# One tile for the residual instead of two, read with a stride by the gather, and an earlier load into the tile that comes free

## The reference, cut to what matters

```python
h = rmsnorm(x, attn_norm_g)
x = x + hybrid_mixer(h, ...)          # ends in concat(...) @ w_out, (256, 2048) @ (2048, 2048)
h = rmsnorm(x, ffn_norm_g)
x = x + hier_moe(h, ...)              # router, then for each expert e its tokens:
                                      #   (silu(h @ w_gate[e]) * (h @ w_up[e])) @ w_down[e], weighted
return rmsnorm(x, final_norm_g)
```

## Time and profile before

| what | us |
|---|---|
| median of 3 runs (lowest 1422.26, highest 1424.28) | 1424.24 |
| profiled execution, first to last instruction (the span; this is also its own time as it was kept) | 1421.9 |
| TensorE busy in it | 1220.1 |
| VectorE busy | 489.9 |
| ScalarE busy | 256.4 |

### The profile page before, as it was taken

One profiled execution on the slowest core, in us unless ns is written; L12 is line 12 of the kernel. 1 busy time (PEld: TensorE's weight loads), 2 busy tenths in 40 slices (PEclk: granted clock), 3 DMA queues, 4 the chain that ended last, 5 costly groups with the idle time before them and its releaser, 6 DMA issues.

```text
span 1421.9 us, 18013 instructions
## 1 busy us (share of the span) xinstructions
PE 1220.1 (86%) x7475; PEld 711.4 (50%) x7475; DVE 489.9 (34%) x1013; ACT 256.4 (18%) x629; POOL 18.3 (1%) x84
## 2 busy tenths in 40 slices
PE   8999999999999998769689958769687686876976
PEld 7999999776568753223244314214242242422422
DVE  5599987663875431121110220111101111011113
ACT  3001111444600132011111102002020020200212
POOL 2000000000010000000000000000000000000001
PEclk9999999999999999789899988979889898898999
DMA  9958567431644899999999999999999999999996
GB/s 300 323 176 173 152 151 238 118 86 34 178 108 163 352 410 428 428 428 427 428 426 429 427 428 428 428 428 427 428 428 428 426 428 428 427 427 428 427 428 261
DMA packets 133363, 479.35 MB, mean 337 GB/s; under 512 B 47804, under 2 KB 105632, under 8 KB 107552
## 3 DMA queue, kind: packets, MB, share of 16 engines
q1 hardware_dynamic: 126816, 477.58, 86.2%
q10 hardware_dynamic: 6464, 0.58, 0.4%
HBM read 476.05 MB, written 2.10 MB: 336 GB/s over the span
## 4 chain that ended last, share of the span: by engine, by line
PE 55%; DMA 42%; DVE 1%; ACT 1%; issue 1%; POOLq 0%; POOL 0%; ACTq 0%; DVEq 0%
DMA ring<-in_expert_w_up_dram 35%; PE PS L1136 14%; PE PS L1456 10%; DMA spare<-in_expert_w_up_dram 6%; PE PS L1278 5%; PE PS L1443 4%; PE PS L1178 3%; PE PS L1255 2%; PE PS L1646 2%; PE PS L1434 1%; PE PS L1230 1%; PE PS L1656 1%; PE PS L956 1%; PE PS L1128 1%; PE PS L1197 1%; PE PS L1518 1%
## 5 line engine op out<-in xcount | busy, mean ns | idle before, releaser
L1456 PE MATMUL PS<-ring,XG 128*32 128x512 f32 x1296 | 231.2, 758 | 131.8 <-DMA ring<-in_expert_w_up_dram 91.3
L1456 PEld LDWEIGHTS PS<-ring,XG 128*32 128x32 f32 x1296 | 57.5, 134 | 264.5 <-issue 261.3
L2904 DVE TENSOR_TENSOR x<-PS,x 128x1024 f32<-128x1024 f32 x41 | 50.2, 1225 | 221.1 <-PE PS L1535 219.8
L3088 DVE TENSOR_TENSOR hTe<-PS,sg 128x128 f32<-128x128 f32 (+1 forms) x31 | 9.9, 319 | 337.5 <-ACT sg L2206 337.3
L1443 PE MATMUL PS<-ring,XG 128*64 128x512 f32 x192 | 93.2, 643 | 18.2 <-DMA ring<-in_expert_w_up_dram 14.8
L2193 ACT ACTIVATE Hs<-PS 128x512 f32<-128x512 f32 x30 | 17.9, 597 | 463.2 <-PE PS L1456 338.9
L1445 PE MATMUL PS<-ring,XG 128*64 128x512 f32 x192 | 93.4, 644 | 0.0
L1535 PE MATMUL PS<-Y,SW 128*128 128x512 f32 (+2 forms) x176 | 90.7, 627 | 1.5 <-ACT ro L2302 1.5
L1456 PE MATMUL PS<-spare,XG 128*32 128x512 f32 x208 | 69.8, 833 | 22.8 <-DMA ring<-in_expert_w_up_dram 22.8
L1434 PEld LDWEIGHTS PS<-sel,xn 128*128 128x128 f32 x640 | 75.3, 191 | 12.9 <-issue 12.7
L1136 PE MATMUL PS<-hT,ring 128*128 128x128 f32 x672 | 78.8, 275 | 0.0
(11 more groups left out here) (497 smaller groups left out, 1576.3 us busy)
## 6 DMA issues: line engine op xcount, KB each, us to landing
ring<-in_expert_w_up_dram SPq DMA_DIRECT2D x53, 2048.0 KB, 23.2
ring<-in_expert_w_gate_dram SPq DMA_DIRECT2D x53, 2048.0 KB, 26.7
ring<-in_expert_w_down_dram SPq DMA_DIRECT2D x51, 2048.0 KB, 25.0
ring<-in_w_in_dram SPq DMA_DIRECT2D x17, 2048.0 KB, 12.3
spare<-in_expert_w_gate_dram SPq DMA_DIRECT2D x9, 2048.0 KB, 24.1
spare<-in_expert_w_up_dram SPq DMA_DIRECT2D x8, 2048.0 KB, 22.7
spare<-in_expert_w_down_dram SPq DMA_DIRECT2D x8, 2048.0 KB, 26.6
ring<-in_w_in_dram SPq DMA_DIRECT2D x16, 512.0 KB, 7.3
```

What stands on the lines that cost most here:

```text
L1456: mm = pe.matmul(PS[r:r + 32, 0, :], gathered_rows(q, 4 * c + j)[:, column:column + 32], weight_rows(slots[u], 4 * (c % 2) + j), start=(c ...
L2904: dve.tensor_tensor(y, new, old, ALU.add).then_inc(sc_added, 1)
```

## The change

1. `xn` is gone, and with it the eight `normed` copies, the semaphore `xn_ready` and the waits for it on TensorE and in the SP list.
2. A tile `xr` of 2 x 2048 floats takes its place in memory. x is loaded into `xr` the second time, in natural order, and the output projection is added to it there. Square sums, router transposes and the first additions of expert results read `xr`.
3. The gather reads `xr` through `token_rows(t, k)`: the same 128 values as before, now with a stride of eight floats. The overflow path does the same; it has no work with these inputs.
4. The loads: block 0 of x is issued when all scores are done (`scored`, 24 of them), since it lies over the queries; block 1 when all weighted sums are done (`pv_done`). Between the two, after `p_turned`, chunk 3 of the second expert step goes into `x1`, which is no longer needed until the additions. The entry near the router goes away, and its waits for `xn_ready` and `ffn_ssq`; `logits_done` stays.
5. The first additions of expert results read their old value from `xr` without a permutation. The tile that the warming products read is `xr`.

```diff
+SCORED = sum(HPG * (t + 1) for p, t in STEPS)
...
-        xn = sb("xn", [P, TT, DK, P])
+        xr = sb("xr", [P, TT, D])
...
+        def token_rows(t, k):
+
+            first = 1024 * (k // 8)
+            return xr[:, t, first + k % 8:first + 1024:8]
...
                 else:
+                    sp.wait_ge(scored, SCORED)
+                    sp.dma_start(xr[:, 0, :], x[0, 0:P, :]).then_inc(x_again, 16)
                     sp.wait_ge(p_turned, 2 * PAIRS_BY[-1])
-                    for t in range(TT):
-                        sp.dma_start(x1[:, t, :], x[0, t * P:(t + 1) * P, :]).then_inc(x_again, 16)
+                    load_chunk(E - STATIC + 1, 1, 3)
+                    sp.wait_ge(pv_done, PAIRS_BY[-1])
+                    sp.dma_start(xr[:, 1, :], x[0, P:2 * P, :]).then_inc(x_again, 16)
                     sp.wait_ge(out_done, TT)
...
             load_half(1, 1)
-            sp.wait_ge(xn_ready, 4 * TT)
             sp.wait_ge(logits_done, 1)
-            sp.wait_ge(ffn_ssq, 4 * TT)
             load_half(2, 1)
             load_early(roww_flat[:, 0:512], 1024)
-            load_chunk(E - STATIC + 1, 1, 3)
...
-            warm = xn[:, 0, 0:4, :].rearrange("p k n -> p (k n)")
+            warm = xr[:, 0, 0:512]
...
                             mm = pe.transpose(PS[:, 2 + f, (j % 2) * T + t * P:(j % 2) * T + (t + 1) * P],
-                                              x1[:, t, 512 * m + j:512 * (m + 1):4], ident[:, :])
+                                              xr[:, t, 512 * m + j:512 * (m + 1):4], ident[:, :])
...
             route_last()
-            pe.wait_ge(xn_ready, 4 * TT)
             keep_warm(4, 4, tile=warm)
...
-                        mm = pe.matmul(PS[:, 6 + f % 2, (k % 2) * P:(k % 2) * P + rows_of_group(q)], xn[:, t, k, :],
+                        mm = pe.matmul(PS[:, 6 + f % 2, (k % 2) * P:(k % 2) * P + rows_of_group(q)], token_rows(t, k),
                                        sel[:, t, 0:rows_of_group(q)], start=(t == 0), stop=(t == TT - 1))
...
-            def normed(m, t):
-
-                k, p = 8 * (m // 2), 64 * (m % 2)
-                dve.tensor_copy(xn[:, t, k:k + 8, p:p + 64].rearrange("t j p -> t p j"),
-                                x1[:, t, m * 512:(m + 1) * 512].rearrange("t (p j) -> t p j", j=8)).then_inc(xn_ready, 1)
...
-                dve.tensor_tensor(x1[:, t, 0:512], PS[:, v, :], x1[:, t, 0:512], ALU.add).then_inc(out_added, 1)
-                dve.wait_ge(out_added, v + 1)
-                normed(0, t)
+                dve.tensor_tensor(xr[:, t, 0:512], PS[:, v, :], xr[:, t, 0:512], ALU.add).then_inc(out_added, 1)
...
-                first = not added_by_part(n, t, cols)
-                if first:
-                    y = y.rearrange("t (p j) -> t p j", j=8)
-                    old = xn[:, t, 8 * cols:8 * cols + 8, :].rearrange("t j p -> t p j")
+                if not added_by_part(n, t, cols):
+                    old = xr[:, t, cols * 1024:(cols + 1) * 1024]
                     held = SLOT_OF.index(RESIDUAL)
                     dve.wait_ge(w_used[held % CHUNKS], held // CHUNKS + 1)
```

More of the change, by code:

```diff
@@ L540, in build @@
         ffn_root = sem("ffn_root")
-        xn_ready = sem("xn_ready")
         xn_turned = sem("xn_turned")
@@ L1429, in gather @@
                         if q == 0:
-                            mm = pe.matmul(PS[:, 6 + f % 2, (k % 2) * P:(k % 2) * P + P], xn[:, t, k, :],
+                            mm = pe.matmul(PS[:, 6 + f % 2, (k % 2) * P:(k % 2) * P + P], token_rows(t, k),
                                            sel[:, t, 0:64].unsqueeze(1).broadcast_to([P, 2, 64]),
@@ L1793, in overflow @@
                                     mm = pe.matmul(PS[:, 6 + f % 2, (k % 2) * 256:(k % 2) * 256 + SLOTS],
-                                                   xn[:, t, k, :], sel[:, t, 0:SLOTS],
+                                                   token_rows(t, k), sel[:, t, 0:SLOTS],
                                                    start=(t == 0), stop=(t == TT - 1))
@@ L2153, in _ @@
                     act.wait_ge(ffn_ssq, v)
-                act.activation(Hs[:, :], x1[:, t, m * 512:(m + 1) * 512], ACT.Square,
+                act.activation(Hs[:, :], xr[:, t, m * 512:(m + 1) * 512], ACT.Square,
                                bias=ZERO_C, accum_out=ssq[:, t, m:m + 1]).then_inc(ffn_ssq, 1)
@@ L2782, in _ @@
                 done = PRODUCTS_BEFORE + 7 * (m - 1)
-                quarters = x1[:, :, 512 * m:512 * (m + 1)].rearrange("p t (h n) -> p t h n", h=2)
+                quarters = xr[:, :, 512 * m:512 * (m + 1)].rearrange("p t (h n) -> p t h n", h=2)
                 of = [PS[:, 4 + n // 2, 256 * (n % 2):256 * (n % 2) + 256] for n in range(7)]
@@ L2805, in _ @@
                 dve.tensor_tensor(quarters[:, 0, 1, :], of[4], quarters[:, 0, 1, :], ALU.add).then_inc(part_added, 1)
-                dve.wait_ge(out_added, TT * m + 1)
-                normed(m, 1)
                 if m < 3:
@@ L2816, in _ @@
                 dve.tensor_tensor(quarters[:, 0, 1, :], of[6], quarters[:, 0, 1, :], ALU.add).then_inc(out_added, 1)
-                dve.wait_ge(out_added, TT * (m + 1))
-                normed(m, 0)
                 if m < 3:
@@ L2901, in add_scattered @@
                 new = PS[:, bank:bank + 2, :].rearrange("p a b -> p (a b)")
-                if first:
-                    new = new.rearrange("t (p j) -> t p j", j=8)
                 dve.tensor_tensor(y, new, old, ALU.add).then_inc(sc_added, 1)
```

## The result

The changed kernel takes 1441.82 us (median of 4 runs, 1441.21 to 1442.42), the kernel before 1423.49 in the runs beside it: ratio 1.0130, interval 1.0118 to 1.0141. That is 18.3 us slower, and outside the range of the prediction.

The account below looks back on a forecast made before the run. TensorE was taken to bound up to about 550 us, then the weight stream. From a span of 1421.9, minus 1.4 for the chunk plus 0.55 for the gather gave 1421.05, so a median of 1423.4 us; range 1419.2 to 1427.0.

Parts of the forecast that it names:

- The gather with a stride: First 32 gather matmuls, before the load at 505.65: strided weight loads cost 17 ns more each, 0.55 us in all.
- own sign of being wrong: The prediction called itself wrong if gather weight loads took 260 ns or more; it expected about 210.
- upper bound of 69 ns: First 32 gather weight loads: at most 69 ns more each, 2.2 us, if the strided reading adds to the 112.
- between two and four the price went up by half: Argument for full-price strided weight loads: reading gets dearer between strides of two and four floats, with no row at eight.
- rival 2: Gather where TensorE leads: strided loads add full price, 69 ns each, 1428.5 us; at 112 ns, 1436; chance 0.18.
- Two regimes, changing over near 550; later gathers hidden: Whole kernel: TensorE sets stage ends up to about 550 us, then the 428 GB/s weight stream, which hides later gathers.
- New place of the chunk: 0: Chunk issued at 384.44 lands by 393.1, block 1 of x about 396, 14 us before need: 0 us.
- The old place: Near the router the queue runs empty at 504.3; the next load lands at 510.35: 1.4 us gained, not 4.9.
- The lead lasts to 551: From the first expert loads to 551 us: the stream's 0.85 us lead stays, narrowly, since later loads find non-empty queues.
- slack of 1.9 us: Load at 512.86 took 6.6 us against 4.7 from an empty queue: 1.9 us to cover 0.8 + 0.85.
- VectorE's copies and additions: 0: Eight copies (5.0 us) go and four additions shorten (3.3 us in all), none on the path: gain 0.

Follow-up runs that it names:

- the seven hidden groups: Changed kernel with the stride of eight only in the gathers outside the first two and the wide expert's two groups, neighbouring floats elsewhere: 1423.05 us, ratio 1.0000.
- side by side kernel: Changed kernel whose gather reads 128 neighbouring floats of the residual tile instead of a stride of eight (other columns): 1423.32 us, ratio 1.0004.
- 10.5 alone: Changed kernel with the stride of eight only in the gathers of the first two groups of experts, neighbouring floats elsewhere: 1433.37 us, ratio 1.0072.
- 7.2 alone: Changed kernel with the stride of eight only in the gathers of the wide expert's two groups, neighbouring floats elsewhere: 1430.08 us, ratio 1.0050.

## Why the prediction was wrong

The step that failed is **"The gather with a stride"**: "If the reading sets a pace of 0.129 at eight floats too, each costs 17 ns more". The pace was 0.238 in place of 0.129, the price 126 ns in place of 17 and 4.0 us in place of 0.55 for the first 32 loads. The prediction's own sign of being wrong, loads of 260 ns or more, came with 335. Two things were wrong in the step. The row that gave 0.129 is of transposes, and the loads measured by themselves show that transposes keep their pace at strides of one to eight, so that row could say nothing of a product's load. And the upper bound of 69 ns came from the same row; it bounded nothing. The trace of before could have warned of it. It has transposes at a stride of two as well, of the same tile that the products of L1466 read at two:

```profile
L1468 PEld LDWEIGHTS PS<-ident,Hs x32: 194/202/209, 664.8 to 1347.1; 128*128 128x128 f32 x32
```

That is 62 ns more than the 140 side by side, at a stride at which a product's load pays 4. So the prediction's "between two and four the price went up by half" rests on rows of two kinds, a product at two and transposes at four. The only row of the gather's own kind was the stride of two, 196 against 192. It was right, and it lies on the free side of the step. The 112 ns of rival 2, "twice as slow as side by side", was the better bound (0.238 / 0.112 = 2.1); its time, 1436, was outside the range that I gave, and the measured 1441.8 lies beyond it too.

The other steps, in the order of the prediction:

- *Two regimes, changing over near 550; later gathers hidden.* Right: 56 us of TensorE in the seven hidden groups cost nothing. But the place moved with the price: in the changed kernel TensorE leads until 582.99.
- *New place of the chunk: 0.* Right: landed at 393.4 and 396.4 (predicted 393.1 and 396).
- *The old place: a hole, so that 1.4 us are gained and not 4.9.* Right in kind. The load into the empty queue took 5.0 us, not 4.7, which with the loads side by side gives 511.75 - (505.77 + 5.0), and 0.12 us more since that execution runs later: 1.1 us.
- *The lead lasts to 551.* Not borne out: in the side by side kernel the load of 551.91 lands after 15.95 us, 0.25 us ahead of the earlier trace rows with the same 0.12. It was gone long before. The load of 505.77 lands 1.1 us ahead, but the one of 512.98 takes 6.4 us where the one of 512.86 took 6.6, and lands 0.2 ahead; from there on the lead stays at 0.2 to 0.3. So the slack of 1.9 us that the prediction saw for that load was not there, and why isn't shown. What was left is too small to be told from nothing.
- *VectorE's copies and additions: 0.* Right: gone or shorter (2037 to 1224 ns), and the side by side kernel takes the time of before.
- *The places where a dearer load would show (rival 2).* Right in kind, and low with the price put in: 128 x 0.126 - 7.5 = 8.6 us for the first two groups (9.8 in the trace, 10.5 alone) and 72 x 0.126 - 3.0 = 6.1 for the wide expert (7.9 in the trace, 7.2 alone). The loads in question show where the rest is. The load that went out at 551.78 now goes out at 568.86 and takes 9.3 us, not the 8.7 of an empty queue, so it lands 568.86 + 9.3 - 567.98 - 0.88 = 9.3 us late. And at the wide expert a later load decides than the prediction took, the one of 790.55 behind 96 gather loads; it now goes out at 813.40. Its landing in the kernel before (KB, us), then issues and landings of both in the changed kernel:

```profile
ring<-in_expert_w_up_dram SPq DMA_DIRECT2D x1, 2048.0 KB, 14.1
```
```profile
568.86 0.33 SPq L694 DMA_DIRECT2D ring<-in_expert_w_up_dram  x1
...
813.40 0.33 SPq L694 DMA_DIRECT2D ring<-in_expert_w_up_dram  x1
```
```profile
ring<-in_expert_w_up_dram SPq DMA_DIRECT2D x1, 2048.0 KB, 9.3
ring<-in_expert_w_up_dram SPq DMA_DIRECT2D x1, 2048.0 KB, 9.2
```

It lands 813.40 + 9.2 - 790.55 - 14.1 = 17.9 us later, of which 0.88 and the 9.8 of the first place are not its own: 7.3 us, where 96 x 0.126 - (14.1 - 8.7) = 6.7. The working was there, except for that load; it was the chance, 0.18, and the end of the range that ignored it.

What stays open: why the loads of transposes keep their pace, and the last 0.5 to 1.2 us of each place, between these loads (9.3 and 6.7) and what was measured.

## What to carry to other kernels

Before an operand of TensorE gets a stride, find a row of the same kind of instruction at that stride; a transpose's load doesn't price a product's. Up to two float32 of stride were free here, and from four on the loads came at half their pace, so a layout copy off the path (here 5.0 us of VectorE) can be worth more than the tile it needs. Where a resource may change its price in steps and no row lies beyond the step, no nearby row bounds the price; the range has to reach at least what the dearest rival gives (here 1436), and a short run of the instruction by itself at the stride in question gives the row that is missing.

## What the runs showed of the hardware

- The step of the price lies between two and four floats for the stationary operand (192, 197, 263, 330, 336, 312 ns at strides 1, 2, 3, 4, 8, 16) and for the moving operand alike (378, 388, 632, 639 ns for 256 columns at 1, 2, 4, 8). The Trainium skill, "SBUF — State Buffer", section "Door 1: The DMA port swizzle (why `[64,N]` ≈ `[32,N]`)", says both that two hits on a line of 16 bytes hide the access and that four floats of stride are free. The first agrees with every product row: stride two has two values on a line, four, eight and sixteen have one, and three, with one or two, lies between (263 ns). The second does not: 330 ns at four against 192.
- Rows of 4 KiB in place of 16 KiB for each partition lowered the rate of the weight stream from 428 to 414 GB/s.
- A load of 1 MiB into an empty queue took 5.0 us in the changed kernel (issued at 510.59) and in the side by side one (505.77), where the row of x had given 4.7.
